# RWKV chunk inverse by doubling: next power and running inverse from one 128-column product per level, in place of two 64-column products

## Chip, cores, metric

One core of one Trainium2 chip. The metric is the device time of one execution in microseconds: before the change 6218.73 us, the median of three runs (6207.51 to 6225.07). All data is float32.

## What is computed

One layer of a diffusion backbone: modulated RMSNorm, a mixing part with two branches (RWKV-7 and HGRN2), an expert part, a final norm. 640 tokens: 512 latent ones in rows of 64 and 128 of context. The change touches the RWKV-7 branch alone, whose recurrence is, for each head of 64 channels and for both directions of time:

```python
def step(s, inp):
    r_t, w_t, k_t, v_t, kk_t, a_t = inp
    sa = jnp.einsum('bhvk,bhk->bhv', s, -kk_t)
    s = (s * w_t[:, :, None, :] + sa[..., None] * (kk_t * a_t)[:, :, None, :]
         + v_t[..., None] * k_t[:, :, None, :])
    return s, jnp.einsum('bhvk,bhk->bhv', s, r_t)
```

## The kernel before, in words

The kernel is a row of stages; `stage_rwkv` is one of them. It goes through the 16 heads in 8 rounds of two heads (a pair fills the 128 partitions), in each round through both directions `d`, and cuts the 640 tokens into 10 chunks of L = 64. Inside a chunk the recurrence needs the inverse of a unit triangular matrix, one 64x64 matrix per head and chunk. With N its strictly triangular part, the inverse is (I + N)(I + N^2)(I + N^4)..., so it is built by squaring N and multiplying into a running product TT, in LEVELS = 5 steps.

Chunks are handled in three groups, GROUPS = ((0, 4), (4, 4), (8, 2)). A matrix is held in two forms: "bd" (128x128, the two heads' blocks on the diagonal, used as the stationary operand) and compact (128x64). A matmul needs its stationary operand transposed, so N is held both ways: bdN and its transpose bdNT. bdN shares its memory with bdTT and carries that name in the profile.

One direction runs like this (line numbers of the profile):
- Gram part (L592 to L608 on PE): per group, products of the factors into banks 4, 5 and 6; DVE masks them into bdNT, TTc, RbT, bdAk, RkT and cN (L869 to L875); two sets of transposes through bank 7, copied out by ACT (L763).
- Levels (L611 to L633): per level and group, PE squares, cN against bdNT (L619), into a bank per group (GB = 4, 5, 6); DVE spreads the square to bdN with the block mask (L879); PE multiplies it into the running product (L625), which DVE adds to TTc (L882); ACT copies the compact form out of bdN, one copy per head, to cN (L769); PE transposes bdN (L631), all groups in bank 7 in turn, and ACT copies the result to bdNT (L772). The last level has neither cN nor transposes.
- DVE spreads TTc to bdTT (L884), and the scan over the chunks begins with the transpose of the initial state (L638).

Each engine runs its own instructions in the order written, and waits on semaphores. To keep PE from idling at these waits, `fill(n)` (from L549) inserts n products of the projections of the next tiles (L546, 320 columns each); a round has 7 x 32 = 224 of them. In the last round only the first 128 exist, so that direction 1 of it has none in its levels.

```python
                        for g, (c0, n) in enumerate(GROUPS):
                            k = 15 * d + 3 * i + g + 1
                            W("bdn_ready", k, r)
                            for c in range(c0, c0 + n):
                                mm = nc.tensor.matmul(tt_view(g, n)[:, c - c0, :], flat(bdN, c), TTc[:, c, :], start=True, stop=True)
                            inc(mm, "tt_sums")
                            if not top:
                                if g:
                                    W("bdnt_ready", 12 * d + 3 * i + g, r)
```

The last two lines are the wait by which group 1's transposes wait for ACT's copy of group 0 out of bank 7, and group 2's for group 1's.

Of the kernel before, what the change touches and what calls it, by code (L numbers as in the profile page):

```python
# [12 lines left out]
P = 128  # L13
# [371 lines left out]
def stage_rwkv(nc, I, O, S, per):  # L385

    with ExitStack() as ctx:
# [20 lines left out]
        cV, RbT, RkT, TTc, cN = (sb(n, [P, NCH, L]) for n in ("cV", "RbT", "RkT", "TTc", "cN"))  # L409
        bdAk, bdTT, bdNT = (sb(n, [P, NCH, 2, L]) for n in ("bdAk", "bdTT", "bdNT"))  # L410
        bdN = bdTT
# [16 lines left out]
        def sq_view(g, n):  # L428
            return ps[:, GB[g], 0:n * L].rearrange("p (c l) -> p c l", l=L)

        def tt_view(g, n):
            return ps[:, GB[g], n * L:2 * n * L].rearrange("p (c l) -> p c l", l=L)
# [101 lines left out]
        def _(pe):  # L534
# [16 lines left out]
            def body(r, last):  # L551
# [29 lines left out]
                for d in range(2):  # L581
# [29 lines left out]
                    for i in range(LEVELS):  # L611
                        top = i == LEVELS - 1
                        for g, (c0, n) in enumerate(GROUPS):
                            if i:
                                W("bdnt_ready", 4 * 3 * d + 3 * (i - 1) + g + 1, r)
                                W("cn_ready", 2 * (12 * d + 3 * (i - 1) + g + 1), r)
                                W("tt_ready", 15 * d + 3 * (i - 1) + g + 1, r)
                            for c in range(c0, c0 + n):
                                mm = nc.tensor.matmul(sq_view(g, n)[:, c - c0, :], flat(bdNT, c), cN[:, c, :], start=True, stop=True)  # L619
                            inc(mm, "squared")  # L620
                        for g, (c0, n) in enumerate(GROUPS):
                            k = 15 * d + 3 * i + g + 1
                            W("bdn_ready", k, r)
                            for c in range(c0, c0 + n):
                                mm = nc.tensor.matmul(tt_view(g, n)[:, c - c0, :], flat(bdN, c), TTc[:, c, :], start=True, stop=True)  # L625
                            inc(mm, "tt_sums")
                            if not top:
                                if g:
                                    W("bdnt_ready", 12 * d + 3 * i + g, r)
                                for c in range(c0, c0 + n):  # L630
                                    mm = nc.tensor.transpose(tr_view(g, n)[:, c - c0, :], flat(bdN, c), ident)  # L631
                                inc(mm, "n_turned")
                            fill(2 if g == 0 else 1)  # L633
                    fill(3)
# [75 lines left out]
        def _(act):  # L710
# [22 lines left out]
            def body(r, last):  # L733
# [11 lines left out]
                for d in range(2):  # L745
# [18 lines left out]
                    for i in range(LEVELS - 1):  # L764
                        for g, (c0, n) in enumerate(GROUPS):
                            W("bdn_ready", 15 * d + 3 * i + g + 1, r)
                            for h in range(2):
                                q = slice(L * h, L * h + L)
                                inc(A(cN[q, c0:c0 + n, :], bdN[q, c0:c0 + n, h, :], ACT.Copy), "cn_ready")  # L769
                        for g, (c0, n) in enumerate(GROUPS):  # L770
                            W("n_turned", 12 * d + 3 * i + g + 1, r)
                            inc(A(bdNT[:, c0:c0 + n].rearrange("p c g l -> p c (g l)"), tr_view(g, n), ACT.Copy), "bdnt_ready")  # L772
# [27 lines left out]
        def _(dve):  # L800
# [5 lines left out]
            with dve.Fori(0, PAIRS) as r:  # L806
# [31 lines left out]
                for d in range(2):  # L838
                    mT, mI, mN = (1, 1, 2) if d == 0 else (2, 3, 1)
                    W("lora_taken", 2 * d + 2, r)  # L840
# [24 lines left out]
                    for g, (c0, n) in enumerate(GROUPS):  # L865
# [3 lines left out]
                        link(V.tensor_tensor(bdNT[:, cs], bcast(G1[:, :, 0:L], 2, 2), bcast(C["bd"][:, 2 + mT], n, 1), ALU.mult))  # L869
                        link(V.tensor_tensor(TTc[:, cs], G1[:, :, 0:L], bcast(C["cm"][:, 2 * d], n, 1), ALU.mult))  # L870
                        link(V.tensor_tensor(TTc[:, cs], TTc[:, cs], bcast(C["ci"][:, :], n, 1), ALU.add))
                        link(V.tensor_tensor(RbT[:, cs], G1[:, :, L:P], bcast(C["cm"][:, mI], n, 1), ALU.mult))
                        link(V.tensor_tensor(bdAk[:, cs], bcast(G2[:, :, 0:L], 2, 2), bcast(C["bd"][:, mT], n, 1), ALU.mult))
                        link(V.tensor_tensor(RkT[:, cs], G2[:, :, L:P], bcast(C["cm"][:, mI], n, 1), ALU.mult))
                        did(V.tensor_tensor(cN[:, cs], G3, bcast(C["cm"][:, 2 - 2 * d], n, 1), ALU.mult), "grams_taken")  # L875
                    for i in range(LEVELS):
                        for g, (c0, n) in enumerate(GROUPS):
                            W("squared", 15 * d + 3 * i + g + 1, r)
                            did(V.tensor_tensor(bdN[:, c0:c0 + n], bcast(sq_view(g, n), 2, 2), bcast(blk, n, 1), ALU.mult), "bdn_ready")  # L879
                        for g, (c0, n) in enumerate(GROUPS):  # L880
                            W("tt_sums", 15 * d + 3 * i + g + 1, r)
                            did(V.tensor_tensor(TTc[:, c0:c0 + n], TTc[:, c0:c0 + n], tt_view(g, n), ALU.add), "tt_ready")  # L882
# [1019 lines left out]
def build_layer(nc, I, O, per=None):  # L1902
# [32 lines left out]
PER = {'bd_factors': 4,  # L1935
 'bdn_ready': 30,
 'bdnt_ready': 24,
# [5 lines left out]
 'cn_ready': 48,  # L1943
# [46 lines left out]
 'n_turned': 24,  # L1990
# [13 lines left out]
 'squared': 30,  # L2004
# [6 lines left out]
 'tt_sums': 30,  # L2011
# [3 lines left out]
 'vector_line': 86,  # L2015
# [30 lines left out]
```

How the kernel before makes its waits and increments, by code:

```python
        @block.sync  # L106
# [23 lines left out]
            assert n + 1 == 18  # L130
            w = I["ada_w"][0].rearrange("(k p) n -> p k n", p=P)
            for r in range(RING):
                sp.dma_start(ring[r][:, :, :], w[:, :, r * CT * P:(r + 1) * CT * P]).then_inc(s_ada[r], 16)
                if r == RING - 1:
                    for t in range(TT):
                        src = I["x_sample"][0, t * P:(t + 1) * P, :] if t < TT - 1 else I["x_prompt"][0]
                        sp.dma_start(xt[:, t, :], src).then_inc(s_x, 16)
            with sp.Fori(1, NBLK // RING) as i:
                for r in range(RING):
                    sp.wait_ge(s_adaf[r], i)
                    sp.dma_start(ring[r][:, :, :], w[:, :, bass.ds((i * RING + r) * (CT * P), CT * P)]).then_inc(s_ada[r], 16)
# [6 lines left out]
            def link(ins):  # L148
                steps[0] += 1
                ins.then_inc(s_id, 1)
                pool.wait_ge(s_id, steps[0])
# [6 lines left out]
        @block.tensor  # L158
        def _(pe):
            ident = S["consts"]["ident"]
            pe.wait_ge(s_id, 2)
            pe.wait_ge(s_par, 18 * 16)
            for t, n in enumerate((128, 126, 72)):
                mm = nc.tensor.transpose(ps[:, 4 + t, 0:n], rows[0:n, t, :], ident[0:n, 0:n])
            mm.then_inc(s_ptr, 1)
            pe.wait_ge(s_cond, 1)
            with pe.Fori(0, NBLK // RING) as i:
                for r in range(RING):
                    pe.wait_ge(s_ada[r], i * 16 + 16)
```

## Time and profile before

| | us |
|---|---|
| median of three runs | 6218.73 |
| lowest, highest run | 6207.51, 6225.07 |
| profiled execution, span from first to last instruction | 6210.8 |
| PE busy | 5735.1 |
| DVE busy | 1991.0 |
| ACT busy | 777.2 |

### The profile page before, as it was taken

The numbers are of one execution on the slowest core, as the hardware profiler recorded it, in microseconds if no ns is written. First come the engines' busy times: TensorE is split into PE (matmuls) and PEld (weight loads), VectorE is DVE, ScalarE is ACT, GpSimd is POOL, SyncE is SP. The second block draws the span as 40 slices with busy tenths as digits, with TensorE's granted clock in tenths as the row PEclk, the third lists the DMA queues.
The fourth block names the chain that finished last, engine by engine and source line by source line (L and its number), as shares of the span: only waits on it lengthen the run. The fifth ranks groups of instructions, "written<-read, shape, count | busy, mean of one in ns | idle before, by whom it ended". The sixth has DMA issues, their size and how long they took to land. (4 is left out here: it accounts for less than half of the span.)

```text
span 6210.8 us, 62442 instructions
## 1 busy us (share of the span) xinstructions
PE 5735.1 (92%) x24221; PEld 3645.7 (59%) x24221; DVE 1991.0 (32%) x3746; ACT 777.2 (13%) x1514; POOL 140.8 (2%) x123
## 2 busy tenths in 40 slices
PE   8989999999999999889999969999799999999997
PEld 1147877778777777767777756676533334334333
DVE  0013455554545555415545441102101101101104
ACT  1002222222212222200010000001000000000001
POOL 0000000000000000000000000000000000000000
PEclk9989999999999999889999979998799999999999
DMA  9821111110111110021111113321485684684782
GB/s 338 308 72 47 33 38 34 43 34 28 37 32 38 34 43 27 7 64 52 51 54 45 31 65 96 110 55 34 163 291 196 205 287 171 231 285 169 249 284 108
DMA packets 435775, 697.30 MB, mean 112 GB/s; under 512 B 18446, under 2 KB 290132, under 8 KB 417108
## 3 DMA queue, kind: packets, MB, share of 16 engines
q1 hardware_dynamic: 435540, 693.98, 33.6%
q8 instruction: 170, 2.79, 0.2%
q14 instruction: 65, 0.53, 0.0%
HBM read 671.39 MB, written 22.54 MB: 112 GB/s over the span
## 5 line engine op out<-in xcount | busy, mean ns | idle before, releaser
L546 PE MATMUL psR<-hT,wrkv 128*128 128x320 f32 x3584 | 1087.4, 442 | 53.3 <-issue 36.9
L546 PEld LDWEIGHTS psR<-hT,wrkv 128*128 128x128 f32 x3584 | 650.6, 193 | 268.7 <-issue 57.6
L1060 PE MATMUL psH<-hT,whg 128*128 128x320 f32 x2560 | 723.2, 438 | 21.2 <-DMA whg<-in_w_in 20.3
L1060 PEld LDWEIGHTS psH<-hT,whg 128*128 128x128 f32 x2560 | 483.2, 193 | 209.7 <-DMA whg<-in_w_in 20.9
L1643 PE MATMUL psE<-hT,xg 128*80 128x512 f32 x1280 | 573.3, 608 | 29.6 <-ACT hidT L1733 23.0
L1643 PEld LDWEIGHTS psE<-hT,xg 128*80 128x80 f32 x1280 | 195.3, 154 | 395.8 <-issue 382.8
L172 PE MATMUL psA<-ada,cond 128*2 128x512 f32 x768 | 333.8, 598 | 13.6 <-DMA ada<-in_ada_w 10.9
L1643 PE MATMUL psE<-mergedT,xg 128*80 128x512 f32 x768 | 334.8, 592 | 0.0
L1794 DVE SCALAR_TENSOR_TENSOR hid<-hid,psE 80x512 f32<-80x512 f32 x32 | 20.5, 680 | 944.3 <-ACT hid L1728 944.3
L1328 PE MATMUL psM<-branches,wmg 128*128 128x320 f32 x1024 | 282.0, 436 | 39.4 <-DMA wmg<-in_w_br_hgrn 29.9
L1665 PE MATMUL psE<-hT,hidT 128*80 128x512 f32 x640 | 279.6, 596 | 11.0 <-DVE x1a L1813 4.6
L1398 PE MATMUL psO<-mergedT,wout 128*128 128x320 f32 x1024 | 281.0, 435 | 8.5 <-DMA wout<-in_w_out 8.5
L1328 PEld LDWEIGHTS psM<-branches,wmg 128*128 128x128 f32 x1024 | 194.7, 191 | 126.7 <-issue 44.7
L1398 PEld LDWEIGHTS psO<-mergedT,wout 128*128 128x128 f32 x1024 | 195.9, 192 | 90.9 <-DMA wout<-in_w_out 9.0
L1643 PEld LDWEIGHTS psE<-mergedT,xg 128*80 128x80 f32 x768 | 115.2, 150 | 214.4 <-issue 214.4
L172 PEld LDWEIGHTS psA<-ada,cond 128*2 128x2 f32 x768 | 65.5, 85 | 281.3 <-issue 277.6
L625 PEld LDWEIGHTS psR<-TTc,bdTT 128*128 128x128 f32 x1600 | 211.2, 193 | 23.7
L625 PE MATMUL psR<-TTc,bdTT 128*128 128x64 f32 x1600 | 210.5, 271 | 0.0
L1665 PEld LDWEIGHTS psE<-hT,hidT 128*80 128x80 f32 x640 | 95.1, 151 | 189.9 <-issue 184.1
L619 PEld LDWEIGHTS psR<-cN,bdNT 128*128 128x128 f32 x1600 | 190.4, 192 | 17.3 <-issue 5.9
L619 PE MATMUL psR<-cN,bdNT 128*128 128x64 f32 x1600 | 189.7, 274 | 1.3 <-DVE cN L875 1.3
L1805 DVE COPY mergedT<-psE 64x512 f32<-64x512 f32 x32 | 21.9, 684 | 523.0 <-PE psE L1665 522.5
(331 smaller groups left out, 6274.8 us busy)
## 6 DMA issues: line engine op xcount, KB each, us to landing
ada<-in_ada_w SPq DMA_DIRECT2D x24, 4096.0 KB, 13.0
hT<-in_moe_w_gate SPq DMA_DIRECT2D x96, 1024.0 KB, 4.8
hT<-in_moe_w_down SPq DMA_DIRECT2D x80, 1024.0 KB, 4.9
hT<-in_moe_w_up SPq DMA_DIRECT2D x64, 1024.0 KB, 4.8
mergedT<-in_moe_w_up SPq DMA_DIRECT2D x64, 1024.0 KB, 4.8
wrkv<-in_w_in SPq DMA_DIRECT2D x56, 1024.0 KB, 6.0
mergedT<-in_moe_w_down SPq DMA_DIRECT2D x48, 1024.0 KB, 4.8
whg<-in_w_in SPq DMA_DIRECT2D x40, 1024.0 KB, 6.0
```

The costliest lines, as they stand in the source:

```text
L172: mm = nc.tensor.matmul(ps[0:2, r, :], cond[:, k, :], ring[r][:, k, :], start=(k == 0), stop=(k == KT - 1))
L546: mm = nc.tensor.matmul(ps[:, BANK[i] + h, 0:HALF], w[:, SLOT[i], k, :], S["hT"][:, k, h * HALF:(h + 1) * HALF], start=(k == 0), stop=(k = ...
L619: mm = nc.tensor.matmul(sq_view(g, n)[:, c - c0, :], flat(bdNT, c), cN[:, c, :], start=True, stop=True)
L625: mm = nc.tensor.matmul(tt_view(g, n)[:, c - c0, :], flat(bdN, c), TTc[:, c, :], start=True, stop=True)
L1060: mm = nc.tensor.matmul(ps[:, 2 * (i % 2) + h, 0:HALF], w[:, i, k, :], S["hT"][:, k, h * HALF:(h + 1) * HALF], start=(k == 0), stop=(k == ...
L1328: mm = nc.tensor.matmul(ps[:, 4 * s + 2 * g + h, 0:HALF], w[s][:, PAIRS * g + k, :], br[:, g, k, h * HALF:(h + 1) * HALF], start=(k == 0), ...
L1398: mm = nc.tensor.matmul(ps[:, 2 * (j % 2) + h, 0:HALF], w[j % 2][:, k, :], mT[:, k, h * HALF:(h + 1) * HALF], start=(k == 0), stop=(k == K ...
L1643: mm = nc.tensor.matmul(ps[0:M, 2 * g + c, :], xg[:, kt, e, :], w[:, kk * FF + c * 512:kk * FF + (c + 1) * 512], start=(kt == 0), stop=(kt ...
L1665: mm = nc.tensor.matmul(ps[0:M, 4 + c, :], hidT[:, m, :], w[:, c * 512:(c + 1) * 512], start=(m == 0), stop=(m == FT - 1))
L1794: V.scalar_tensor_tensor(out=hid[:, cut], in0=hid[:, cut], scalar=1.0, in1=ps[0:M, c, :], op0=ALU.add, op1=ALU.mult)\
L1805: V.tensor_copy(ys[64 * (e % 2):64 * (e % 2) + 64, c * 512:(c + 1) * 512], ps[0:64, 4 + c, :])
```

## The change

The roles of the two forms are swapped. M, the transpose of N, and TT stand side by side in one buffer MT ([.., 0, :] is cM, [.., 1, :] is TTc), and bdN is the stationary operand. One product of bdN with MT's 128 columns gives the next power of M (left half) and the term to be added to TT (right half). The power is spread by DVE to bdM (which shares its memory with bdTT), transposed by PE, and copied by ACT to bdN. So TT is always one level behind the power, and there are LEVELS + 1 = 6 passes: level 0 has only the left half (64 columns), levels 1 to 4 have 128 columns, level 5 only the right half. Level 4's power is now transposed too. The multiplication that made cN in the gram part is gone. The fill products are 2, 1, 1 after the transposes of each of levels 0 to 4, and 1, 1, 1 after the products of level 5, in place of the three before the scan.

```diff
--- before.py
+++ after.py
@@ -406,9 +406,11 @@
         KR = sb("KR", [P, NCH, 2, L])
         cB = sb("cB", [P, NCH, L])
         bdB, bdK, bdKW, bdBn, bdKn, bdV = (sb(n, [P, NCH, 2, L]) for n in ("bdB", "bdK", "bdKW", "bdBn", "bdKn", "bdV"))
-        cV, RbT, RkT, TTc, cN = (sb(n, [P, NCH, L]) for n in ("cV", "RbT", "RkT", "TTc", "cN"))
-        bdAk, bdTT, bdNT = (sb(n, [P, NCH, 2, L]) for n in ("bdAk", "bdTT", "bdNT"))
-        bdN = bdTT
+        cV, RbT, RkT = (sb(n, [P, NCH, L]) for n in ("cV", "RbT", "RkT"))
+        MT = sb("MT", [P, NCH, 2, L])
+        cM, TTc = MT[:, :, 0, :], MT[:, :, 1, :]
+        bdAk, bdTT, bdN = (sb(n, [P, NCH, 2, L]) for n in ("bdAk", "bdTT", "bdN"))
+        bdM = bdTT
         Sc, bdS, nR, cSA, bdSA = (sb("Sc", [P, 2, L]), sb("bdS", [P, 2, 2, L]), sb("nR", [P, L]), sb("cSA", [P, L]),
                                   sb("bdSA", [P, 2, L]))
         s0 = sb("s0", [P, 2, L])
@@ -425,11 +427,8 @@
             return ps[:, b, 0:n * width].rearrange("p (c l) -> p c l", l=width)
         GB = (4, 5, 6)
 
-        def sq_view(g, n):
-            return ps[:, GB[g], 0:n * L].rearrange("p (c l) -> p c l", l=L)
-
-        def tt_view(g, n):
-            return ps[:, GB[g], n * L:2 * n * L].rearrange("p (c l) -> p c l", l=L)
+        def power_view(g, n, half):
+            return ps[:, GB[g], 0:n * P].rearrange("p (c h l) -> p c h l", h=2, l=L)[:, :, half, :]
 
         def tr_view(g, n):
             return ps[:, 7, 0:n * P].rearrange("p (c l) -> p c l", l=P)
@@ -608,30 +607,31 @@
                         fill(4 if g < 2 else 3)
                     W("grams_taken", 3 * d + 3, r)
                     W("rows_taken", 6 * d + 6, r)
-                    for i in range(LEVELS):
-                        top = i == LEVELS - 1
+                    for i in range(LEVELS + 1):
+                        top = i == LEVELS
                         for g, (c0, n) in enumerate(GROUPS):
                             if i:
-                                W("bdnt_ready", 4 * 3 * d + 3 * (i - 1) + g + 1, r)
-                                W("cn_ready", 2 * (12 * d + 3 * (i - 1) + g + 1), r)
-                                W("tt_ready", 15 * d + 3 * (i - 1) + g + 1, r)
+                                W("bdn_ready", 15 * d + 3 * (i - 1) + g + 1, r)
+                            if 0 < i < LEVELS:
+                                W("cm_ready", 2 * (12 * d + 3 * (i - 1) + g + 1), r)
+                            if i > 1:
+                                W("tt_ready", 15 * d + 3 * (i - 2) + g + 1, r)
+                            lo, hi = (0 if i < LEVELS else L), (P if i else L)
                             for c in range(c0, c0 + n):
-                                mm = nc.tensor.matmul(sq_view(g, n)[:, c - c0, :], flat(bdNT, c), cN[:, c, :], start=True, stop=True)
-                            inc(mm, "squared")
+                                mm = nc.tensor.matmul(ps[:, GB[g], (c - c0) * P + lo:(c - c0) * P + hi], flat(bdN, c), flat(MT, c)[:, lo:hi],
+                                                      start=True, stop=True)
+                            inc(mm, "powers")
                         for g, (c0, n) in enumerate(GROUPS):
-                            k = 15 * d + 3 * i + g + 1
-                            W("bdn_ready", k, r)
+                            if top:
+                                fill(1)
+                                continue
+                            W("bdm_ready", 15 * d + 3 * i + g + 1, r)
+                            if g:
+                                W("bdn_ready", 15 * d + 3 * i + g, r)
                             for c in range(c0, c0 + n):
-                                mm = nc.tensor.matmul(tt_view(g, n)[:, c - c0, :], flat(bdN, c), TTc[:, c, :], start=True, stop=True)
-                            inc(mm, "tt_sums")
-                            if not top:
-                                if g:
-                                    W("bdnt_ready", 12 * d + 3 * i + g, r)
-                                for c in range(c0, c0 + n):
-                                    mm = nc.tensor.transpose(tr_view(g, n)[:, c - c0, :], flat(bdN, c), ident)
-                                inc(mm, "n_turned")
+                                mm = nc.tensor.transpose(tr_view(g, n)[:, c - c0, :], flat(bdM, c), ident)
+                            inc(mm, "m_turned")
                             fill(2 if g == 0 else 1)
-                    fill(3)
                     W("bdtt_ready", 3 * d + 3, r)
 
                     W("s0_spread", d + 1, r)
@@ -761,15 +761,15 @@
                         for m, out in enumerate((bdBn, bdKn)):
                             W("rows_turned", 6 * d + 2 * g + m + 1, r)
                             inc(A(out[:, c0:c0 + n].rearrange("p c g l -> p c (g l)"), bank(7, n, P), ACT.Copy), "rows_taken")
-                    for i in range(LEVELS - 1):
+                    for i in range(LEVELS):
                         for g, (c0, n) in enumerate(GROUPS):
-                            W("bdn_ready", 15 * d + 3 * i + g + 1, r)
-                            for h in range(2):
+                            W("bdm_ready", 15 * d + 3 * i + g + 1, r)
+                            for h in range(2 if i < LEVELS - 1 else 0):
                                 q = slice(L * h, L * h + L)
-                                inc(A(cN[q, c0:c0 + n, :], bdN[q, c0:c0 + n, h, :], ACT.Copy), "cn_ready")
+                                inc(A(MT[q, c0:c0 + n, 0, :], bdM[q, c0:c0 + n, h, :], ACT.Copy), "cm_ready")
                         for g, (c0, n) in enumerate(GROUPS):
-                            W("n_turned", 12 * d + 3 * i + g + 1, r)
-                            inc(A(bdNT[:, c0:c0 + n].rearrange("p c g l -> p c (g l)"), tr_view(g, n), ACT.Copy), "bdnt_ready")
+                            W("m_turned", 15 * d + 3 * i + g + 1, r)
+                            inc(A(bdN[:, c0:c0 + n].rearrange("p c g l -> p c (g l)"), tr_view(g, n), ACT.Copy), "bdn_ready")
                         if i == 0 and d == 0:
                             take_gate(r, 1)
                         if i == 0 and d and not last:
@@ -837,6 +837,7 @@
                 link(V.tensor_tensor(cV[:, :, :], bdV[:, :, 0, :], bdV[:, :, 1, :], ALU.add))
                 for d in range(2):
                     mT, mI, mN = (1, 1, 2) if d == 0 else (2, 3, 1)
+                    assert mN == 3 - mT
                     W("lora_taken", 2 * d + 2, r)
                     link(V.tensor_scalar(t1[:, :], t1[:, :], -0.5 * DECAY_SCALE, -0.5 * DECAY_SCALE, ALU.mult, ALU.add))
                     link(V.tensor_scalar(t3[:, :], t2[:, :], dp[:, 7:8], dp[:, 8:9], ALU.mult, ALU.add))
@@ -866,20 +867,19 @@
                         cs = slice(c0, c0 + n)
                         W("grams", 3 * d + g + 1, r)
                         G1, G2, G3 = bank(4, n, P), bank(5, n, P), bank(6, n, L)
-                        link(V.tensor_tensor(bdNT[:, cs], bcast(G1[:, :, 0:L], 2, 2), bcast(C["bd"][:, 2 + mT], n, 1), ALU.mult))
-                        link(V.tensor_tensor(TTc[:, cs], G1[:, :, 0:L], bcast(C["cm"][:, 2 * d], n, 1), ALU.mult))
-                        link(V.tensor_tensor(TTc[:, cs], TTc[:, cs], bcast(C["ci"][:, :], n, 1), ALU.add))
+                        link(V.tensor_tensor(bdN[:, cs], bcast(G3, 2, 2), bcast(C["bd"][:, 2 + mN], n, 1), ALU.mult))
+                        link(V.tensor_tensor(cM[:, cs], G1[:, :, 0:L], bcast(C["cm"][:, 2 * d], n, 1), ALU.mult))
+                        link(V.tensor_tensor(TTc[:, cs], cM[:, cs], bcast(C["ci"][:, :], n, 1), ALU.add))
                         link(V.tensor_tensor(RbT[:, cs], G1[:, :, L:P], bcast(C["cm"][:, mI], n, 1), ALU.mult))
                         link(V.tensor_tensor(bdAk[:, cs], bcast(G2[:, :, 0:L], 2, 2), bcast(C["bd"][:, mT], n, 1), ALU.mult))
-                        link(V.tensor_tensor(RkT[:, cs], G2[:, :, L:P], bcast(C["cm"][:, mI], n, 1), ALU.mult))
-                        did(V.tensor_tensor(cN[:, cs], G3, bcast(C["cm"][:, 2 - 2 * d], n, 1), ALU.mult), "grams_taken")
-                    for i in range(LEVELS):
+                        did(V.tensor_tensor(RkT[:, cs], G2[:, :, L:P], bcast(C["cm"][:, mI], n, 1), ALU.mult), "grams_taken")
+                    for i in range(LEVELS + 1):
                         for g, (c0, n) in enumerate(GROUPS):
-                            W("squared", 15 * d + 3 * i + g + 1, r)
-                            did(V.tensor_tensor(bdN[:, c0:c0 + n], bcast(sq_view(g, n), 2, 2), bcast(blk, n, 1), ALU.mult), "bdn_ready")
-                        for g, (c0, n) in enumerate(GROUPS):
-                            W("tt_sums", 15 * d + 3 * i + g + 1, r)
-                            did(V.tensor_tensor(TTc[:, c0:c0 + n], TTc[:, c0:c0 + n], tt_view(g, n), ALU.add), "tt_ready")
+                            W("powers", 18 * d + 3 * i + g + 1, r)
+                            if i < LEVELS:
+                                did(V.tensor_tensor(bdM[:, c0:c0 + n], bcast(power_view(g, n, 0), 2, 2), bcast(blk, n, 1), ALU.mult), "bdm_ready")
+                        for g, (c0, n) in enumerate(GROUPS if i else ()):
+                            did(V.tensor_tensor(TTc[:, c0:c0 + n], TTc[:, c0:c0 + n], power_view(g, n, 1), ALU.add), "tt_ready")
                     for g, (c0, n) in enumerate(GROUPS):
                         did(V.tensor_tensor(bdTT[:, c0:c0 + n], bcast(TTc[:, c0:c0 + n], 2, 2), bcast(blk, n, 1), ALU.mult), "bdtt_ready")
                     dve.wait_ge(signal(f"s0_in{d}").sem, r * 16 + 16)
```

The semaphore counts in the table PER are changed to match.

The order of PE's work, one level in the middle (first round, direction 0; MT is cM and TTc, bdTT is bdN before and bdM after; semaphore and register rows are left out). Before:

```order
L619 MATMUL psR<-cN,bdNT 128x64 x4
L619 MATMUL psR<-cN,bdNT 128x64 x4
L619 MATMUL psR<-cN,bdNT 128x64 x2
L625 MATMUL psR<-TTc,bdTT 128x64 x4
L631 MATMUL psR<-ident,bdTT 128x128 x4
L546 MATMUL psR<-hT,wrkv 128x320 x2
L625 MATMUL psR<-TTc,bdTT 128x64 x4
L631 MATMUL psR<-ident,bdTT 128x128 x4
L546 MATMUL psR<-hT,wrkv 128x320
L625 MATMUL psR<-TTc,bdTT 128x64 x2
L631 MATMUL psR<-ident,bdTT 128x128 x2
L546 MATMUL psR<-hT,wrkv 128x320
```

And in the change:

```order
L621 MATMUL psR<-MT,bdN 128x128 x4
L621 MATMUL psR<-MT,bdN 128x128 x4
L621 MATMUL psR<-MT,bdN 128x128 x2
L632 MATMUL psR<-ident,bdTT 128x128 x4
L545 MATMUL psR<-hT,wrkv 128x320 x2
L632 MATMUL psR<-ident,bdTT 128x128 x4
L545 MATMUL psR<-hT,wrkv 128x320
L632 MATMUL psR<-ident,bdTT 128x128 x2
L545 MATMUL psR<-hT,wrkv 128x320
```

The three blocks of running sums between the transposes are gone, and each block of products is 128 columns wide.

PE's last level before, up to the start of the scan:

```order
L619 MATMUL psR<-cN,bdNT 128x64 x4
L619 MATMUL psR<-cN,bdNT 128x64 x4
L619 MATMUL psR<-cN,bdNT 128x64 x2
L625 MATMUL psR<-TTc,bdTT 128x64 x4
L546 MATMUL psR<-hT,wrkv 128x320 x2
L625 MATMUL psR<-TTc,bdTT 128x64 x4
L546 MATMUL psR<-hT,wrkv 128x320
L625 MATMUL psR<-TTc,bdTT 128x64 x2
L546 MATMUL psR<-hT,wrkv 128x320 x4
L638 MATMUL psR<-ident,bdSA 128x128
```

And in the change its last two:

```order
L621 MATMUL psR<-MT,bdN 128x128 x4
L621 MATMUL psR<-MT,bdN 128x128 x4
L621 MATMUL psR<-MT,bdN 128x128 x2
L632 MATMUL psR<-ident,bdTT 128x128 x4
L545 MATMUL psR<-hT,wrkv 128x320 x2
L632 MATMUL psR<-ident,bdTT 128x128 x4
L545 MATMUL psR<-hT,wrkv 128x320
L632 MATMUL psR<-ident,bdTT 128x128 x2
L545 MATMUL psR<-hT,wrkv 128x320
L621 MATMUL psR<-MT,bdN 128x64 x10
L545 MATMUL psR<-hT,wrkv 128x320 x3
L638 MATMUL psR<-ident,bdSA 128x128
```

The last power is turned as well, and ten more products follow it before the scan.

## Rows read from the trace of the kernel before

**Rows 1.** The page: its first line, and each engine's busy time.
```profile
span 6210.8 us, 62442 instructions
...
PE 5735.1 (92%) x24221; PEld 3645.7 (59%) x24221; DVE 1991.0 (32%) x3746; ACT 777.2 (13%) x1514; POOL 140.8 (2%) x123
```

**Rows 2.** Timeline of PE, levels of one direction: start, length, operation [idle before <-releaser]
```profile
1119.85 2.44 PE L619 MATMUL psR<-cN,bdNT 128*128 128x64 f32 x20
...
1127.52 2.34 PE L619 MATMUL psR<-cN,bdNT 128*128 128x64 f32 x20
1129.69 1.06 PE L625 MATMUL psR<-TTc,bdTT 128*128 128x64 f32 x8
...
1132.95 0.61 PE L631 MATMUL psR<-ident,bdTT 128*128 128x128 f32 x4
1133.39 0.70 PE L546 MATMUL psR<-hT,wrkv 128*128 128x320 f32 x2
...
1134.33 0.39 PE L631 MATMUL psR<-ident,bdTT 128*128 128x128 f32 x2
1134.55 0.70 PE L546 MATMUL psR<-hT,wrkv 128*128 128x320 f32 x2
1135.09 2.34 PE L619 MATMUL psR<-cN,bdNT 128*128 128x64 f32 x20
```

**Rows 3.** Timeline of DVE in the level that starts at 1127.52
```profile
1128.56 0.69 DVE L879 TENSOR_TENSOR bdTT<-psR,bdmask 128x512 f32<-128x512 f32 x1 [1.25 <-PE psR L619]
1129.45 1.24 DVE L879 TENSOR_TENSOR bdTT<-psR,bdmask 128x512 f32<-128x512 f32 x2 [0.20 <-PE psR L619]
1130.86 0.42 DVE L882 TENSOR_TENSOR TTc<-TTc,psR 128x256 f32<-128x256 f32 x1 [0.17 <-PE psR L625]
```

**Rows 4.** Timeline of ACT in the same level
```profile
1129.28 2.41 ACT L769 ACTIVATE cN<-bdTT 64x256 f32<-64x256 f32 x6 [1.13 <-DVE bdTT L879]
1131.72 0.60 ACT L772 ACTIVATE bdNT<-psR 128x512 f32<-128x512 f32 x1
```

**Rows 5.** Timeline of PE, last level of the same direction
```profile
1150.24 2.34 PE L619 MATMUL psR<-cN,bdNT 128*128 128x64 f32 x20
...
1156.27 2.37 PE L546 MATMUL psR<-hT,wrkv 128*128 128x320 f32 x8
1159.21 0.33 PE L638 MATMUL psR<-ident,bdSA 128*128 128x128 f32 x1 [0.58 <-DVE bdSA L886]
```

**Rows 6.** Timeline of PE, last round, second direction (no fill left)
```profile
2597.86 3.28 PE L619 MATMUL psR<-cN,bdNT 128*128 128x64 f32 x20 [1.26 <-DVE cN L875]
...
2607.11 2.34 PE L619 MATMUL psR<-cN,bdNT 128*128 128x64 f32 x20
...
2611.96 0.65 PE L631 MATMUL psR<-ident,bdTT 128*128 128x128 f32 x4 [0.33 <-ACT bdNT L772]
...
2613.31 0.44 PE L631 MATMUL psR<-ident,bdTT 128*128 128x128 f32 x2 [0.29 <-ACT bdNT L772]
2613.58 2.34 PE L619 MATMUL psR<-cN,bdNT 128*128 128x64 f32 x20
...
2626.52 2.34 PE L619 MATMUL psR<-cN,bdNT 128*128 128x64 f32 x20
...
2633.89 0.45 PE L638 MATMUL psR<-ident,bdSA 128*128 128x128 f32 x1 [2.79 <-DVE bdSA L886]
```

**Rows 7.** Timeline of PE, gram part of group 1, same direction as rows 2
```profile
1108.92 1.16 PE L597 MATMUL psR<-KR,bdB 128*128 128x128 f32 x8
1109.91 1.06 PE L597 MATMUL psR<-KR,bdK 128*128 128x128 f32 x8
1110.81 1.00 PE L599 MATMUL psR<-cB,bdKW 128*128 128x64 f32 x8
```

**Rows 8.** Timeline of PE early in a round; then windows over it (PEclk near the end)
```profile
1074.70 1.28 PE L577 MATMUL psR<-ident,bdK 128*128 128x128 f32 x10 [1.09 <-DVE t L832]
1076.86 4.10 PE L568 MATMUL psR<-lora,lw 128*128 128x320 f32 x8 [0.87 <-ACT bdV L744]
...
1070.00:1075.00 5.00, 3.91 (x17) 2.56 (x16) 0.92 (x2) 3.38 (x5) 0.00 (x0) 1.00 0.00 0
1075.00:1080.00 5.00, 4.13 (x15) 2.89 (x14) 4.54 (x2) 1.69 (x4) 0.00 (x0) 0.69 0.02 3
```

More of the change, by code:

```diff
@@ L1932, in build_layer @@
         return S
-PER = {'bd_factors': 4,
+PER = {'bdm_ready': 30,
+ 'cm_ready': 48,
+ 'm_turned': 30,
+ 'powers': 36,
+ 'bd_factors': 4,
  'bdn_ready': 30,
- 'bdnt_ready': 24,
  'bdtt_ready': 6,
@@ L1942 @@
  'bonus_sums': 1,
- 'cn_ready': 48,
  'derived': 1,
@@ L1989 @@
  'mixed': 3,
- 'n_turned': 24,
  'nr_ready': 20,
@@ L2003 @@
  'sa_sums': 20,
- 'squared': 30,
  'state_ready': 20,
@@ L2010 @@
  'tt_ready': 30,
- 'tt_sums': 30,
  'v_spread': 2,
@@ L2014 @@
  'var_sums': 1,
- 'vector_line': 86,
+ 'vector_line': 80,
  'y_squares': 1,
```

## The prediction

> **What bounds the kernel now.** I read the page first: TensorE (PE) is busy 92% of the span, VectorE (DVE) 32% and ScalarE (ACT) 13% [rows 1]. That says "PE", but it is a mean over stages. So I went to the timeline of PE inside the stage that the change touches: one round in the middle, first direction, the levels of the chunk inverse. There PE has no idle time at all: the ten squarings start at 1127.52, the next level's at 1135.09, so a level lasts 7.57 us, filled to the end with squarings, running sums, transposes and projection products from `fill` [rows 2]. Then I asked what the same level needs on the other engines, since they run beside it: DVE 1.24 + 0.69 us for the three spreads and then the adds [rows 3], and ACT 2.41 us in one block of six copies before the first copy of a turned matrix [rows 4]. Last I looked for the place where `fill` has run dry. In the last round's second direction no projection product is left, and the same level lasts 6.47 us, with PE waiting twice for ACT's copies [rows 6]. That is the row to remember: with 2.16 us of fill gone the level got only 1.10 us shorter. Under PE's work lies a chain through ACT that is nearly as long.
>
> **Prices of PE's work.** Ten 64-column products take 2.17 us from start to start of the next line, 0.217 each; a fill product of 320 columns takes 0.54; four transposes take 0.44, 0.11 each [rows 2]. The 128-column product is in the trace too, with the same weights: the second block of four in the gram part takes 0.90 us, 0.225 each [rows 7]. So twice the columns cost nothing more. Per column a fill product takes 1.69 ns, so 64 columns would need 0.11 us and 128 columns 0.22: the 64-column product is held by its weight load, and the 128-column one just fills it.
>
> The Trainium skill ("TensorE: Matmul & The Clock Gate", section "Back-to-back issue gap") gives for an isolated matmul a gap that grows with its columns, N/2.4 + 2.5 ns, which would make the 64-column product half as dear as the wide one. By that the merging would save nothing on PE, and the ten transposes more would make a direction 1.1 us longer, an estimate of some 16 us over the kernel. The trace sides with the other sentence of that section, that weight load and matmul set the spacing together.
>
> **The change, part by part** (per direction, of which there are 16; 15 have fill, one has none).
> PE's work: 100 products of 64 columns become 60 products (10 of 64 columns at level 0, 40 of 128 at levels 1 to 4, 10 of 64 in the added level 5), less 40 x 0.217 = 8.7 us; transposes go from 40 to 50, plus 1.1 us. Fill products stay at 23. So PE is relieved of 7.6 us. ACT has three copies of turned matrices more. DVE has one multiplication per group fewer in the gram part.
>
> What becomes of the 7.6 us is decided by the chain, which I follow in one level from the start of its products at 0:
> - group 0's four products end at 0.89, and DVE starts its spread at 1.04, as before [rows 2, 3]; it ends at 1.73;
> - ACT starts at 1.77 its six narrow copies, 2.41 us, to 4.18, and only then the first wide copy, 0.60 us, to about 4.80 [rows 4];
> - all groups are turned in bank 7, so group 1's transposes wait for that copy. In the level without fill they start at 4.85 after the products (2607.11 to 2611.96) [rows 6]. Today there is cover for this time: the running sums of group 0 and group 1 and two fill products. Of it the sums are gone. PE is through with products (2.22), transposes of group 0 (0.44) and two fills (1.08) at 3.74 and idles 1.1 us;
> - group 1's transposes 0.49 us, one fill 0.54, to 5.9; ACT's copy of group 1 ends later, so group 2's transposes start at 6.20 (2613.31 in the level without fill) [rows 6], idle 0.3; they take 0.27;
> - one fill product, 0.54, and then the next level's products: 7.05 us.
> The level's price goes from 7.57 to 7.05, not to 5.5, which PE's work alone would give. Without fill it stays at 6.47.
>
> Level 4 has no narrow copies, in the change either. There ACT takes each turned matrix at once: 2.22 + 0.44 + 0.21 + 0.60 = 3.47, hidden by the two fills; group 1 turns at 3.74, is copied by 4.99, group 2 turns at 5.05, then a fill: 5.86 us.
> Level 5 is new: ten products, 2.22 us, three fills, 1.62, and the end. Today PE reaches the transpose of L638 2.94 us after its last product was issued (1156.27 to 1159.21) [rows 5]; in this time DVE does the last add and the spreads of the inverse, and that stays. So 2.22 + 2.94 = 5.16, of which PE idles 1.3.
> Sum: 4 x 7.05 + 5.86 + 5.16 = 39.2 us, against 39.36 today (1119.85 to 1159.21) [rows 2, 5]: **-0.15 us**. The whole relief of 7.6 us is eaten by the added level, whose turn, copy and products stand in series, and by gaps.
>
> Gram part: the multiplication that made cN goes, 0.42 us in groups 0 and 1. PE is not idle there, but its first block after the wait takes 0.99 us where the next takes 0.90 [rows 7]: a weight load kept waiting by 0.1 us. I count 0.1 us at each of groups 1 and 2 and at level 0: **-0.3 us**. The gain is no larger because fill covers the rest.
> So 15 x -0.45 = -7 us.
>
> The last round's second direction: levels 0 to 3 stay as they are; the last level was 7.37 us (2626.52 to 2633.89) [rows 6] and becomes level 4 without fill, 2.22 + 0.44 + 0.21 + 0.60 then 0.06 + 0.49 + 0.20 + 0.60 then 0.06 + 0.27 = 5.15, plus 5.16: +2.9 us. There the DVE multiplications do stand on the path, -1.2 us. PE idles there much more than before, and the clock may fall to its lower level for one level more: its first level, run mostly at a low clock, took 9.25 us (2597.86 to 2607.11), 2.8 more than the others [rows 6]. I take one such level: in sum +4 us.
> Total -7 + 4 = **-3 us**. The profiled execution has a span of 6210.8 us [rows 1], within 0.2% of the median of the runs, 6218.73; taken off the median, 6216 us.
>
> **Bounds of what is not in the trace.** An add and a spread that read one half of a 128-column block, and copies that write one half: DVE already reads such halves in the gram part, and I take the durations of today; from below nothing, from above 0.1 us at each of the chain's four hand-overs per level, +0.4 x 4 and 0.1 at the end, 25 us over the kernel. DVE's waits are no longer on the count it has just raised; I take nothing, and the same upper bound holds it.
>
> **Rivals.**
> A. PE's work is the bound, all gaps get filled. For it: no idle time in today's level [rows 2]. Against: the level without fill, where taking 2.16 us of work bought 1.10 [rows 6]. It would give 15 x -7.6 = -114: about 6105 us. Chance 0.04.
> B. The clock falls, on the slower side. PE goes from gapless to some 1.4 us of idle per level, both gaps within its second half. For it: at 1074.70 and 1076.86 PE idled 1.09 and 0.87 us with only ten transposes between, and the granted clock over the next stretch was 0.69, a mix of the 2.4 and 1.2 GHz levels [rows 8]; and a level at a low clock cost 2.8 us more [rows 6]. Against: the gaps of 0.33 and 0.29 in the levels without fill went with levels of 6.47 us each, and the new gaps are split by two fill products. It decides from the point where the 1.4 us of idle are enough; if one level in five of 75 falls, 15 x 2.8 = +42: about 6258 us. Chance 0.09. The Trainium skill (same page, "A second HAM failure mode: psum-queue depth-cycling") tells of frequent short idles between groups of matmuls that make the clock swing; that rule speaks against this change, and no row at a gap of just this size shows it.
> C. The chain is longer than worked out, by the upper bound above: about 6241 us. Chance 0.07.
> D. The chain is shorter by over 1 us a direction (a hand-over hidden, a tail that overlaps): about 6195 us. Chance 0.06.
> The forecast, within a few us of no change, has 0.74.
>
> **How the numbers follow.** A measurement of this kernel can tell about 0.3%, 19 us, from no change. Faster: A and D, 0.10. Slower: B and C, 0.16. Same: 0.74. The range leaves out A, half of D and half of B, and holds the spread of the runs: 6195 to 6250.
>
> **What would show it.** In the changed profile: levels 0 to 3 of about 7.05 us with idle before the transposes of groups 1 and 2, released by ACT's copy of the turned matrix; level 4 of 5.9; a wait of about 1.3 us before L638, released by DVE; PE's busy time down by up to 110 us with the span unchanged. Levels near 5.5 us would make A right; a granted clock under 1 inside the levels of ordinary rounds, B; levels of 7.4 or more at full clock, C.

## The result, and the profile after

The changed kernel takes 6367.72 us (median of four runs, 6336.95 to 6379.11), the kernel before 6213.12 beside it: ratio 1.0244, 95% interval 1.0216 to 1.0271. It is slower by 2.4%; I had said 6216 us and no change. The page of the changed kernel, its first line and the busy times, as [rows 1]:

```profile
span 6375.6 us, 60092 instructions
...
PE 5786.2 (91%) x23101; PEld 3635.1 (57%) x23101; DVE 1973.2 (31%) x3698; ACT 802.4 (13%) x1562; POOL 140.8 (2%) x123
```

PE has 1,120 matmul instructions fewer and is busy for 51 us more. That is the first thing to see: fewer instructions and more time in them suggests that some ran at another clock (the wider products alone cannot be it, see the prices below). So the second view is the windows, laid over the two parts of a direction, first the levels (from the first product to the scan's first transpose) and then the scan. Columns: the stretch, its length, busy time and count of PE, PEld, DVE, ACT, POOL, then PEclk, the share of DMA, GB/s. One direction of the kernel before:

```profile
1119.85:1159.21 39.36, 38.79 (x287) 34.80 (x286) 16.80 (x34) 16.00 (x37) 0.00 (x0) 1.00 0.02 9
1159.21:1191.10 31.89, 30.58 (x206) 27.22 (x207) 12.05 (x43) 2.87 (x11) 0.00 (x0) 1.00 0.15 44
```

And two directions of the changed kernel:

```profile
866.69:907.56 40.87, 33.30 (x218) 26.11 (x217) 16.79 (x34) 17.58 (x40) 0.00 (x0) 1.00 0.02 9
907.56:939.40 31.84, 30.58 (x205) 27.20 (x205) 12.03 (x42) 2.87 (x11) 0.00 (x0) 1.00 0.15 45
1147.96:1188.81 40.85, 33.29 (x217) 26.09 (x215) 16.78 (x34) 17.58 (x40) 0.00 (x0) 1.00 0.02 9
1188.81:1243.10 54.29, 53.11 (x205) 46.70 (x205) 12.03 (x42) 2.87 (x11) 0.00 (x0) 0.52 0.09 26
```

The levels take 40.9 us in both, 1.5 more than before, at the full clock. The scan takes 31.84 us in one, as before, and 54.29 in the other, at a granted clock of 0.52, with the same 205 matmul records. Over all 16 directions: levels 626.6 us before and 655.5 after, scans 516.8 and 653.6. These +28.9 and +136.8 make up the difference of the two spans, 164.8 us, to within 1 us. Of the 15 scans with fill, ten ran partly or wholly at the low clock (34.96 to 54.45 us), where before none did. Three of the ten, of about 54.4 us, stayed low to their end. In the other seven the clock came back inside the scan, after 7 to 41 us. One of these, up to the return and from it on:

```profile
1023.02:1043.72 20.70, 20.34 (x78) 17.79 (x78) 3.98 (x14) 0.89 (x4) 0.00 (x0) 0.51 0.00 1
1043.72:1063.73 20.01, 19.18 (x129) 17.04 (x129) 8.08 (x29) 1.96 (x7) 0.00 (x0) 1.00 0.00 1
```

The timeline of PE over the levels of the direction from 1147.96 on, as [rows 2, 5]:

```profile
1147.96 2.34 PE L621 MATMUL psR<-MT,bdN 128*128 128x64 f32 x20
...
1155.10 2.39 PE L621 MATMUL psR<-MT,bdN 128*128 128x128 f32 x20
1157.33 0.60 PE L632 MATMUL psR<-ident,bdTT 128*128 128x128 f32 x4
1157.76 1.24 PE L545 MATMUL psR<-hT,wrkv 128*128 128x320 f32 x4
1160.09 0.63 PE L632 MATMUL psR<-ident,bdTT 128*128 128x128 f32 x4 [1.08 <-ACT bdN L772]
...
1161.49 0.41 PE L632 MATMUL psR<-ident,bdTT 128*128 128x128 f32 x2 [0.24 <-ACT bdN L772]
...
1162.28 2.39 PE L621 MATMUL psR<-MT,bdN 128*128 128x128 f32 x20
...
1176.66 2.39 PE L621 MATMUL psR<-MT,bdN 128*128 128x128 f32 x20
...
1182.85 2.34 PE L621 MATMUL psR<-MT,bdN 128*128 128x64 f32 x20
1185.03 1.83 PE L545 MATMUL psR<-hT,wrkv 128*128 128x320 f32 x6
1188.81 0.33 PE L638 MATMUL psR<-ident,bdSA 128*128 128x128 f32 x1 [1.95 <-DVE bdSA L886]
...
1190.51 1.38 PE L545 MATMUL psR<-hT,wrkv 128*128 128x320 f32 x2
1191.69 0.53 PE L666 MATMUL psR<-nR,bdTT 128*128 128x64 f32 x2
```

A level lasts 7.18 us (1155.10 to 1162.28), the first 7.14, level 4 6.19 and level 5 5.96. The transposes of group 1 wait 1.08 us and those of group 2 0.24 us for ACT's copy. Before L638 PE waits 1.95 us, where it was 0.58 [rows 5], and 1.7 us later a fill product takes 1.18 us from start to start in place of 0.6: the clock has gone to its 1.2 GHz level. In this direction it stays there through the scan. The last step of the same scan, and the first block after it:

```profile
1240.80 0.64 PE L668 MATMUL psR<-Sc,ident 128*128 128x64 f32 x2
1241.23 0.63 PE L669 MATMUL psR<-KR,bdS 128*128 128x64 f32 x2
1241.66 0.63 PE L671 MATMUL psR<-cSA,bdBn 128*128 128x64 f32 x2
...
1243.40 2.34 PE L545 MATMUL psR<-hT,wrkv 128*128 128x320 f32 x4
```

The products of the scan start 0.43 us apart, where they were 0.22. Here the clock comes back only in the long block of 320-column products behind (the granted clock of 1248 to 1252 is 0.93).

### The profile page after: what moved, and what is told of

It reads as the page before. It is cut to its first block and busy times, and to the rows that moved or that the text cites. A ratio compares the mean times of both kernels' runs of the same rounds, so it can differ in the third digit from the quotient of the medians.

```text
span 6375.6 us, 60092 instructions
## 1 busy us (share of the span) xinstructions
PE 5786.2 (91%) x23101; PEld 3635.1 (57%) x23101; DVE 1973.2 (31%) x3698; ACT 802.4 (13%) x1562; POOL 140.8 (2%) x123
## 5 line engine op out<-in xcount | busy, mean ns | idle before, releaser
L545 PE MATMUL psR<-hT,wrkv 128*128 128x320 f32 x3584 | 1152.1, 461 | 51.1 <-issue 35.4
L545 PEld LDWEIGHTS psR<-hT,wrkv 128*128 128x128 f32 x3584 | 675.1, 202 | 266.3 <-issue 59.8
L880 DVE TENSOR_TENSOR bdTT<-psR,bdmask 128x512 f32<-128x512 f32 (+1 forms) x240 | 144.7, 603 | 314.5 <-PE psR L621 304.9
L621 PEld LDWEIGHTS psR<-MT,bdN 128*128 128x128 f32 x1920 | 232.9, 195 | 15.5 <-DVE RkT L875 1.2
L621 PE MATMUL psR<-MT,bdN 128*128 128x128 f32 (+1 forms) x1920 | 232.0, 277 | 0.9 <-DVE RkT L875 0.9
L632 PE MATMUL psR<-ident,bdTT 128*128 128x128 f32 x800 | 132.6, 281 | 97.1 <-ACT bdN L772 95.9
L632 PEld LDWEIGHTS psR<-ident,bdTT 128*128 128x128 f32 x800 | 88.3, 143 | 171.4 <-issue 169.8
```

Of the source, the lines that this page charges most:

```text
L545: mm = nc.tensor.matmul(ps[:, BANK[i] + h, 0:HALF], w[:, SLOT[i], k, :], S["hT"][:, k, h * HALF:(h + 1) * HALF], start=(k == 0), stop=(k = ...
L621: mm = nc.tensor.matmul(ps[:, GB[g], (c - c0) * P + lo:(c - c0) * P + hi], flat(bdN, c), flat(MT, c)[:, lo:hi], start=True, stop=True)
L880: did(V.tensor_tensor(bdM[:, c0:c0 + n], bcast(power_view(g, n, 0), 2, 2), bcast(blk, n, 1), ALU.mult), "bdm_ready")
```

## Experiments

Theory T: PE's wait before the scan lets the clock fall, and the scan keeps it low. Rival R: the repeated gaps inside the levels do it. Both were stated before the runs, and so was what each edit would give. "Fill" means the 320-column products; "dense" work follows itself without a gap, and the scan is called thin since most of its products have 64 columns and it begins with a gap of 0.47 us. Each ratio is against the kernel before as it ran beside the edit: 6225.48 us for the first four, 6214.46 for the last three.

**The wait alone, in the kernel before.** No merged product here; the three fill products that stood before the scan go to the gram part.

```diff
-                        fill(4 if g < 2 else 3)
+                        fill(5 if g < 2 else 4)
...
-                    fill(3)
                     W("bdtt_ready", 3 * d + 3, r)
```

> The kernel before, with one thing moved: the three fill products that stood before the scan go to the gram part, one to each group. PE's work is the same; PE now waits some 2.2 us before the scan's first transpose (0.58 of before plus 1.62) and nowhere else anew; the levels stay gapless. Theory T (the wait before the scan is what lets TensorE's clock fall, and the scan then stays at the low clock): scans at a clock of about 0.5 in ten or more of the 15 directions with fill, the kernel near 6370 us. Rival R (the many gaps inside the levels bring the clock down): no scan falls; only the bare wait is paid, 15 x 1.6 = 24 us, so about 6237 us.

6319.77 us, ratio 1.0170 (1.0128 to 1.0212). The timeline of PE at the end of the first direction's levels:

```profile
620.07 0.33 PE L637 MATMUL psR<-ident,bdSA 128*128 128x128 f32 x1 [2.19 <-DVE bdSA L885]
```

The wait is 2.19 us. The levels are as gapless as before and take 39.27 us. Eleven of 15 scans have a clock under 1, and the scans cost 79 us more than before. More than half of the change's damage (79 of 137 us in the scans) is there without the change: T holds, and R, which had no scan fall, does not. As many scans fell as I had said (ten or more), but for shorter, at 0.59 to 0.90 over a scan and not 0.5; hence 6320 and not 6370. In five of the eleven the clock fell before the scan's first transpose, so within the wait. In one of them, the wait from its start up to the fall, and then the stretch at the low clock:

```profile
1892.65:1894.50 1.85, 0.00 (x0) 0.00 (x0) 1.75 (x4) 0.00 (x0) 0.00 (x0) 1.00 0.00 0
1894.52:1904.74 10.22, 9.59 (x36) 8.25 (x36) 1.83 (x7) 0.45 (x2) 0.00 (x0) 0.50 0.00 0
```

The scan's first transpose starts at 1894.83. Moving the fill makes the wait and takes the wide products from in front of the scan at once; no run parts the two.

**The wait covered, in the changed kernel.** Six fill products in level 5, taken from the end of the round.

```diff
                             if top:
-                                fill(1)
+                                fill(2)
                                 continue
...
-                fill(14)
+                fill(8)
```

> The changed kernel, with the three fill products of level 5 doubled to six and six fewer at the end of the round (8 for 14). The gaps inside the levels stay as they are (1.08 and 0.24 us each); the wait before the scan shrinks from 1.95 to about 0.35 us. Theory T: no scan falls; levels stay 40.9 us a direction, the total is before +22 us for the levels, less 1.6 x 15 = 24 for products that now lie in the gap: about 6215 us. Rival R: the scans still fall, about 6350 us.

6229.69 us, ratio 1.0008 (0.9998 to 1.0017). PE before the scan:

```profile
1159.09 3.45 PE L545 MATMUL psR<-hT,wrkv 128*128 128x320 f32 x12
1162.88 0.33 PE L638 MATMUL psR<-ident,bdSA 128*128 128x128 f32 x1 [0.34 <-DVE bdSA L886]
```

The wait is 0.34 us, and all 15 scans run at 1.00 in 31.8 to 31.9 us, although the levels keep their gaps and their 40.85 us. That is 138 us off the changed kernel's median from six products a round moved. It is 15 us more than I had expected. Between the profiled spans it is 17 us over the kernel before, where I had -2. Ten of the difference lie in the last round's second direction, which has no fill left: its levels take 45.81 us with a clock of 0.76, for 36.03 before. The rest, outside levels and scans, gives back 15 us where I had 24, since the wait at the next round's start grows from 5.88 us to this:

```profile
1061.65 1.96 PE L545 MATMUL psR<-hT,wrkv 128*128 128x320 f32 x3 [8.05 <-issue]
```

The clock is low behind this wait as well, and for longer. PE's first stretch after it, in the kernel before and here:

```profile
1059.82:1063.27 3.45, 3.45 (x7) 2.27 (x8) 3.02 (x7) 0.00 (x0) 0.00 (x0) 0.50 0.12 38
1061.65:1066.75 5.10, 5.10 (x10) 3.30 (x11) 4.43 (x12) 0.00 (x0) 0.00 (x0) 0.50 0.16 43
```

**The gaps in the levels removed, the wait left.** ACT copies a group's turned matrix right after that group's narrow copies.

```diff
                                 inc(A(MT[q, c0:c0 + n, 0, :], bdM[q, c0:c0 + n, h, :], ACT.Copy), "cm_ready")
-                        for g, (c0, n) in enumerate(GROUPS):
                             W("m_turned", 15 * d + 3 * i + g + 1, r)
```

> The changed kernel, with ACT's order inside a level changed: per group the narrow copies and then at once the wide copy of the turned matrix, in place of all narrow ones first. The gaps inside the levels nearly go (about 0.3 us left of 1.3), a level takes about 5.9 to 6.0 us for 7.18; level 4 about 5.9 for 6.19; the wait of 1.95 us before the scan stays. Theory T: the levels save 15 x 4.9 = 73 us but the scans still fall as often: about 6290 us. Rival R: the scans do not fall: 6368 - 73 - 137 = about 6160 us.

6308.84 us, ratio 1.0129 (1.0089 to 1.0169). A level:

```profile
1146.28 2.39 PE L621 MATMUL psR<-MT,bdN 128*128 128x128 f32 x20
1148.51 0.60 PE L632 MATMUL psR<-ident,bdTT 128*128 128x128 f32 x4
1148.94 1.24 PE L545 MATMUL psR<-hT,wrkv 128*128 128x320 f32 x4
1150.02 0.60 PE L632 MATMUL psR<-ident,bdTT 128*128 128x128 f32 x4
...
1151.40 0.41 PE L632 MATMUL psR<-ident,bdTT 128*128 128x128 f32 x2 [0.24 <-ACT bdN L771]
...
1152.19 1.05 PE L621 MATMUL psR<-MT,bdN 128*128 128x128 f32 x8
```

5.91 us for 7.18, and only 0.24 us of wait left; the levels of a direction take 35.5 us. The wait before the scan is again 1.95 us, and 12 of 15 scans ran with a lowered clock, 167 us over the undisturbed ones. This is the mirror image of the run before: levels nearly without gaps and falling scans, there levels with gaps and no falls. It also shows what held the level: the order of ACT's copies, as I had followed it, worth 5.3 us a direction.

**A shorter wait.** DVE adds group by group in level 5; in the changed kernel it waits for all three groups' products before the first add.

```diff
-                        for g, (c0, n) in enumerate(GROUPS):
+                        for g, (c0, n) in enumerate(GROUPS if i < LEVELS else ()):
                             W("powers", 18 * d + 3 * i + g + 1, r)
...
                         for g, (c0, n) in enumerate(GROUPS if i else ()):
+                            if i == LEVELS:
+                                W("powers", 18 * d + 3 * i + g + 1, r)
```

> The changed kernel, where DVE in level 5 waits for a group's products and adds them at once, instead of waiting for all three groups first. The wait before the scan shrinks from 1.95 to about 1.2 us, level 5 takes 5.2 us for 5.96. Theory T: 12 us less for the waits themselves, and fewer scans at the low clock, since 1.2 us is nearer to the 0.58 of before, where none fell: 6215 to 6300 us. Rival R: as many falls as before this edit, about 6356 us.

6314.85 us, ratio 1.0146 (1.0072 to 1.0220). The levels take 40.03 us, 0.8 less. Nine of 15 scans still fell, but for shorter: 64 us over the undisturbed ones for 137. The time lies a little above T's range; the runs spread by 91 us. The profiled execution took 6289.54 us, and two of the others, 6340.16 and 6348.92, lie near R's number, so this run does not settle whether a wait of 1.1 us makes fewer scans fall.

**The wait left, dense work behind it.** Three fill products right after the first sum of the scan, six fewer at the end of the round.

```diff
                     first_sum(0)
+                    fill(3)
...
-                fill(14)
+                fill(8)
```

> The changed kernel, its wait of 1.95 us before the scan left as it is, with three fill products put after the scan's first transpose and first sum (six fewer at the end of the round): 1.6 us of gapless work right behind the wait, where the scan's first gap of 0.47 us lies. If the wait alone is enough to bring the clock down: scans fall as before, near 6360 us. If it takes the wait and the thin start of the scan together: few or none fall, near 6230 us.

6245.45 us, ratio 1.0052 (1.0036 to 1.0069). Three of 15 scans fell, and each came back within a few us, 34.5 us for 32.8. One of the three:

```profile
1285.54 0.30 PE L638 MATMUL psR<-ident,bdSA 128*128 128x128 f32 x1 [1.95 <-DVE bdSA L887]
...
1285.85 2.43 PE L545 MATMUL psR<-hT,wrkv 128*128 128x320 f32 x6
1288.07 0.52 PE L660 MATMUL psR<-Sc,bdKW 128*128 128x64 f32 x2
...
1290.39 0.33 PE L667 MATMUL psR<-nR,bdTT 128*128 128x64 f32 x2
1290.56 0.39 PE L669 MATMUL psR<-Sc,ident 128*128 128x64 f32 x2
```

The fill block runs into the low clock at first, and from 1290.39 on the products are back at full speed, 0.17 us to the next product. So neither answer holds alone: with a wait of 1.95 us the clock can fall although dense work follows (three of 15), but mostly it takes the thin start of the scan with it (ten of 15 in the changed kernel). With the fill behind the wait each low stretch lasted about 3.4 us; without it, behind the same wait, 7 to 58 us. What makes it short or long among scans with the same instructions stays open.

**Two edits, then three.** First the adds and the fill together:

> The changed kernel with two of the three edits: DVE adds group by group in level 5 and six fill products there; ACT's order as in the changed kernel. Levels of 7.18 us with their gaps stay. Theory T: no scan falls; a direction's levels take 40.3 us, 0.5 less than with the fill edit alone: 15 x 0.5 = 8 us less than its 6230, about 6222 us. It parts the gain of the three edits together into ACT's order (the difference to that run) and the rest.

6220.38 us, ratio 1.0006 (0.9995 to 1.0018), no scan falls, 40.36 us a direction. Then ACT's order too:

> The changed kernel with all three edits: ACT copies a group's turned matrix right after its narrow copies, DVE adds group by group in level 5, six fill products in level 5 in place of three (six fewer at the end of the round). Theory T: no scan falls; a direction's levels take 35.0 us (35.5 as with the ACT edit alone, less 0.5 at the end) for 39.4 before; six products moved off the end of the round gave 2.4 us a round in the earlier run. Per round 2 x 4.4 + 2.4 = 11 us, eight rounds 88, less some 5 for the last: about 6140 us against 6225. Rival R2 (the level's chain cannot be shortened for long since the clock falls whatever stands before the scan): above 6225.

6131.25 us, ratio 0.9871 (0.9854 to 0.9887): 1.3% faster than the kernel before, and the best of all. PE at the end of level 5:

```profile
1129.90 3.45 PE L545 MATMUL psR<-hT,wrkv 128*128 128x320 f32 x12
1133.19 0.27 PE L638 MATMUL psR<-ident,bdSA 128*128 128x128 f32 x1
```

PE reaches the scan without a wait; all 15 scans take 31.8 us, the levels 35.04 for 39.36. Of the 87.5 us between this profiled span and that of the kernel before, 65 lie in the levels. So the merged products do pay once their relief is not spent on waiting: ACT's order on top of the two other edits brings 89 us (6220 to 6131). The kernel before was not run with ACT's new order; its levels with fill had no idle time that the order could take away [rows 2], so that it would gain little there is argued, not shown.

## Why the prediction was wrong

- **Prices of PE's work: right.** Ten 128-column products take 2.23 us (1155.10 to 1157.33), ten of 64 columns 2.18. Merging costs nothing per product. A gap that grows with the columns, which would have made the wide product nearly twice as dear, does not show.
- **The chain of a level: right in kind, 0.13 us short.** 7.05 predicted, 7.18 measured (the terms as I listed them, 6.20 + 0.27 + 0.54, add up to 7.01, so 0.17 is missing from them). The waits before the transposes stand where I put them (1.1 and 0.3; 1.08 and 0.24).
- **Level 4: 5.86 predicted, 6.19 measured.** I let ACT copy group 0's turned matrix as soon as it is there. But ACT first goes through its waits for all three spreads, even with no narrow copy to make. DVE's last two spreads, and ACT's first copy:

```profile
1178.64 1.24 DVE L880 TENSOR_TENSOR bdTT<-psR,bdmask 128x512 f32<-128x512 f32 x2 [0.20 <-PE psR L621]
```

```profile
1179.91 0.60 ACT L772 ACTIVATE bdN<-psR 128x512 f32<-128x512 f32 x1 [3.21 <-DVE bdTT L880]
```

 ACT starts only when the third spread is through (1178.64 + 1.24).
- **Level 5: the step that failed first.** I wrote 2.22 + 2.94 = 5.16, "of which PE idles 1.3", with DVE's adds of groups 0 and 1 beside PE's products. It was 5.96, with 1.95 idle. In the changed code DVE waits for all three groups before its first add, so all three stand behind the products:

```profile
1185.23 1.19 DVE L882 TENSOR_TENSOR MT<-MT,psR 128x256 f32<-128x256 f32 x3 [4.12 <-PE psR L621]
1186.46 1.88 DVE L884 TENSOR_TENSOR bdTT<-MT,bdmask 128x512 f32<-128x512 f32 x3
1188.47 0.29 DVE L886 TENSOR_TENSOR bdSA<-s,bdmask 128x128 f32<-128x128 f32 x1
```

 The edit of that loop took the 0.8 us back. These three sizes together are about 1.6 us a direction, some 25 over the kernel. Alone they would have made my 6216 about 6241, still inside my range.
- **The clock: the step that decided.** The sum priced the wait before the scan as bare idle time and put what runs behind it at nothing. It was 137 us. My rival B had the mechanism, with the wrong place and the wrong price. I looked for the fall in the levels, where the gaps repeat, and priced it by a level, 2.8 us. In none of the 15 directions with fill did the levels fall below 1.00. I had 1.3 us of idle before the scan in my own sum and did not ask what stands behind it: a stage of 64-column products that, once slow, costs 3 to 22.6 us, since the clock came back inside it only after 7 to 41 us, or not at all. The evidence lay in [rows 8], two waits with a thin stretch between. The rule of frequent short idles (the Trainium skill, "TensorE: Matmul & The Clock Gate", section "A second HAM failure mode: psum-queue depth-cycling") is no better guide in these 15: gaps of 1.08 and 0.24 us in every level left the clock at 1.00. The sixteenth direction, without fill, is the exception. Its levels, with more idle time, had the clock go down, up and down again, as that rule has it, and then left it at 1.00 for 23.84 us of which PE was busy for 12.26:

```profile
2757.21:2767.45 10.24, 8.12 (x38) 7.38 (x38) 2.51 (x5) 4.68 (x11) 0.00 (x0) 0.50 0.00 0
2767.45:2770.86 3.41, 1.37 (x11) 0.92 (x9) 1.90 (x5) 2.12 (x6) 0.00 (x0) 1.00 0.01 2
2770.86:2774.28 3.42, 2.76 (x13) 2.79 (x14) 0.35 (x1) 0.90 (x2) 0.00 (x0) 0.50 0.00 0
2774.28:2798.12 23.84, 12.26 (x101) 10.89 (x100) 11.68 (x25) 9.28 (x21) 0.00 (x0) 1.00 0.00 1
```

 Two of the gaps in that last stretch are longer than the 1.95 us before the scan, 2.16 us and this one, and the clock stayed up:

```profile
2784.72 0.63 PE L632 MATMUL psR<-ident,bdTT 128*128 128x128 f32 x4 [2.17 <-ACT bdN L772]
```

 So the length of a wait does not tell by itself whether the clock falls.

- **Gram part: right.** From the end of the first scan to the second direction's levels it takes 42.73 us for 43.05, -0.3 as I had it.
- **Last round: nearly right.** Levels of 42.39 us for 36.03 in its second direction, +6.4 where I had 2.9 + 2.8, at a granted clock of 0.84 for 0.90.

## What to carry to other kernels

When work is taken off a busy TensorE, list every wait that loses its cover, and for each one what runs behind it: here a wait of 1.95 us before a stage of 64-column products cost up to eleven times itself in clock, while gaps of 1.08 and 0.24 us inside the levels, between dense blocks, cost only themselves wherever the levels had fill. Move a few covering products into such a wait before judging the change. And when products are merged, look at the engine that copies between them: here merging brought nothing even without falls (6220 us, ratio 1.0006), and the order of the copies made it pay.

## What was not expected of the hardware

- After a wait of 1.95 us the scan ran at the low clock for up to 54 us although PE was busy for 53.11 of 54.29 us. So a busy PE did not by itself bring the clock back in the three longest scans; the fill block behind them did. In seven others it came back inside the scan, and no run shows why there.
- After the same wait the scans took different times in directions with the same instructions (31.84, 34.96, 40.68 and 54.29 us in one execution), so a single execution says little about such a kernel; the runs of the kernels with falls spread over 42 to 91 us (the kernel with the wait left and dense work behind it apart), those of the two edits without falls that keep ACT's order over 6. Falls are not all of it: the kernel before, in whose scans with fill none was seen, spread over 23 and 28 us.
- Where a fill product stands before it, PE's transposes started 0.14 us after ACT's copy (1160.09 after 1159.95), against 0.05 in the level without fill of the kernel before (2611.96 after 2611.91) [rows 6]. This makes up most of the 0.13 us by which the level was longer. Whether the fill product is the reason was not tested.
